# Final read and write of a fused two-block transformer kernel: residual tiles read without the last looped expert block, whose rows become a ninth tile

## What is computed

```python
x = x + gate_f * hierarchical_moe(h, ...)     # x before this: x3, [1024, 1024]
return rms_norm_2(x, final_g)

def hierarchical_moe(h, ...):                 # 2 of 32 experts for each token
    ...
    def run_block(args):                      # 128 slots of one expert
        tok, e = args
        xb = hf[jnp.minimum(tok, n_tok - 1)]
        return (jax.nn.silu(xb @ w_gate[e]) * (xb @ w_up[e])) @ w_down[e]
    out = lax.map(run_block, ...) * slot_gate
    return jnp.zeros((n_tok, dm)).at[slot_tok].add(out, mode='drop')
```

## Time and profile before

| what | us |
|---|---|
| median of 3 runs | 2104.06 (2104.06 to 2104.1) |
| the profiled execution | 2103.95 |
| its span | 2102.3 |
| TensorE busy | 2024.2 (96%) |
| VectorE busy | 1704.6 (81%) |
| ScalarE busy | 1232.5 (59%) |
| GpSimd busy | 445.4 (21%) |
| TensorE ends its last matmul | 2088.3 |

### The profile page before, as it was taken

How to read it: one execution, slowest core, us unless ns; L and a number is a source line. 1 busy time by engine, 2 the same in 40 slices (tenths; PEclk the granted TensorE clock), 3 DMA queues, 4 the chain that set the end, 5 groups by cost and what they waited for, 6 DMA issues and landing times.

```text
span 2102.3 us, 31575 instructions
## 1 busy us (share of the span) xinstructions
PE 2024.2 (96%) x9692; PEld 1673.5 (80%) x9692; DVE 1704.6 (81%) x1922; ACT 1232.5 (59%) x1438; POOL 445.4 (21%) x368
## 2 busy tenths in 40 slices
PE   5999999969999999999999999999999999999997
PEld 4888887858888888888788787888888888887874
DVE  6676756588999999999856455668999999999995
ACT  5311103226888888888644532224888888888874
POOL 2000001101000000100010353111444444444433
PEclk9999999969999999999999999999999999999999
DMA  9476754259999999999722112356999999999997
GB/s 353 142 235 227 253 196 161 110 210 337 390 392 401 392 398 392 400 390 383 280 66 60 32 41 102 119 191 227 386 384 379 375 382 374 363 381 364 380 350 274
DMA packets 201416, 592.52 MB, mean 282 GB/s; under 512 B 23936, under 2 KB 61076, under 8 KB 201341
## 3 DMA queue, kind: packets, MB, share of 16 engines
q1 hardware_dynamic: 177632, 527.50, 66.1%
q0 software_dynamic: 22640, 61.32, 10.1%
q10 hardware_dynamic: 1068, 2.73, 0.4%
HBM read 560.57 MB, written 50.91 MB: 291 GB/s over the span
## 4 chain that ended last, share of the span: by engine, by line
PE 77%; DMA 11%; DVE 8%; ACT 2%; issue 2%; POOL 0%; DVEq 0%; POOLq 0%; SPq 0%; ACTq 0%
PE ps L2467 23%; PE ps L2470 22%; PE ps L2468 22%; DMA ring<-in_w_expert_up 8%; DVE mL L2309 2%; PE ps L2812 1%; DMA ring<-in_ada_w 1%; PE ps L2981 1%; DMA ring<-in_w_expert_down 1%; ACT mH L1440 1%; PE ps L2588 1%; PE ps L2687 1%; DVE mL L2393 1%; PE ps L2676 1%; PE ps L2636 1%
## 5 line engine op out<-in xcount | busy, mean ns | idle before, releaser
L2309 DVE TENSOR_TENSOR mL<-ring,mH 128x1024 fp32r<-128x1024 f32 x384 | 480.8, 1292 | 21.8 <-ACT mH L1440 20.3
L1856 DVE TENSOR_TENSOR mL<-ring,mH 128x1024 fp32r<-128x1024 f32 x384 | 456.5, 1221 | 19.1 <-ACT mH L1231 5.2
L1231 ACT ACTIVATE mH<-ring 128x1024 fp32r<-128x1024 f32 x384 | 401.8, 1060 | 98.1 <-PE ps L2470 87.0
L1440 ACT ACTIVATE mH<-ring 128x1024 fp32r<-128x1024 f32 x384 | 396.4, 1056 | 70.0 <-PE ps L2470 24.3
L2467 PE MATMUL ps<-mH,xsH 128*128 128x512 f32 x1072 | 433.7, 405 | 2.9 <-DVE mL L2309 1.4
L2468 PE MATMUL ps<-mL,xsH 128*128 128x512 f32 x1072 | 418.0, 390 | 0.0
L2470 PE MATMUL ps<-mH,xsL 128*128 128x512 f32 x1072 | 376.8, 391 | 0.0
L2470 PEld LDWEIGHTS ps<-mH,xsL 128*128 128x128 f32 x1072 | 201.2, 188 | 45.0
L2467 PEld LDWEIGHTS ps<-mH,xsH 128*128 128x128 f32 x1072 | 201.7, 188 | 41.6 <-DVE mL L2309 1.6
L2468 PEld LDWEIGHTS ps<-mL,xsH 128*128 128x128 f32 x1072 | 202.0, 188 | 37.3
L948 POOL TENSOR_TENSOR xz<-xz,gate_ffn_row 128x340 f32<-128x340 f32 (+1 forms) x93 | 160.4, 1729 | 242.6 <-DVE mL L2309 216.7
(11 more groups left out here) (487 smaller groups left out, 3151.6 us busy)
## 6 DMA issues: line engine op xcount, KB each, us to landing
ring<-in_w_expert_gate SPq DMA_DIRECT2D x140, 512.0 KB, 12.2
ring<-in_w_expert_up SPq DMA_DIRECT2D x140, 512.0 KB, 12.2
ring<-in_w_expert_down SPq DMA_DIRECT2D x140, 512.0 KB, 12.9
ring<-in_moe_w_gate SPq DMA_DIRECT2D x128, 512.0 KB, 6.6
ring<-in_moe_w_up SPq DMA_DIRECT2D x128, 512.0 KB, 6.5
ring<-in_moe_w_down SPq DMA_DIRECT2D x128, 512.0 KB, 7.8
ring<-in_ada_w SPq DMA_DIRECT2D x96, 512.0 KB, 7.1
ring<-in_sc_w_in SPq DMA_DIRECT2D x24, 512.0 KB, 9.0
```

The source lines that it names most:

```text
L1231: act.activation(mH[:, wset, :], ring[:, slot, :], ACT.Copy).then_inc(S["m1_hi"], 1)
L1440: act.activation(mH[:, wset, :], ring[:, slot, :], ACT.Copy).then_inc(S["m2_hi"], 1)
L1856: dve.tensor_tensor(mL[:, wset, :], ring[:, slot, :], mH[:, wset, :].bitcast(F32), ALU.subtract).then_inc(S["m1_lo"], 1)
L2309: dve.tensor_tensor(mL[:, wset, :], ring[:, slot, :], mH[:, wset, :].bitcast(F32), ALU.subtract).then_inc(S["m2_lo"], 1)
```

## The change

- SyncE waits for the scatter before the last looped block's (`OUT1` without the 16) instead of its own, and reads the eight tiles without those rows.
- GpSimd gathers the last looped block's rows of x3 into `more_rows` (the buffer `gated`), VectorE adds the block's weighted result: the ninth tile. It is squared, its root made, and it is finished in place.
- The scatter into x3 stays, for tokens that are in the rest block too, and waits until all reads have landed (`x_in[t]` at 48).
- `patch(more_rows, tok_out[1])` and then `patch(ys[0], last_tok)` write over rows of `out`, one after the other.
- Finished tiles go to `xz[0]`, `acc`, `ring[0..3]`, `xz[0]`, `acc`, so that `ring[4..11]` keep the rest block's weights; tile 2 waits for the gate product, tiles 6 and 7 for the landing of writes 0 and 1.
- VectorE's `last_hidden` halves move behind tiles 4 and 6, `last_sum` behind all nine finishes; on ScalarE the Silu comes after square 3 and the copies of the hidden halves after square 7.
- The drain of the first looped block goes; one stands before the first gathers, one at the start of step 31.

```diff
-    out_rows = [ring[:, t, :] for t in range(NT)]
+    out_rows = [xz[:, 0, :], acc[:]] + [ring[:, u, :] for u in range(4)] + [xz[:, 0, :], acc[:]]
+    more_rows = gated
...
-        sp.wait_ge(m2_out[1], 16 * blocks + OUT1 + 16)
+        sp.wait_ge(m2_out[1], 16 * blocks + OUT1)
...
+        pool.drain()
         for e in range(2):
             tokens_known(0, e)
             gather2(0, e)
 
         def m2_step(q, r):
             s = 2 * q + r
+            if static(q) and s == E2 - 1:
+                pool.drain()
...
-            if static(b) and b == 0:
-                pool.drain()
             rows_back(b)
...
+        pool.wait_ge(m2_out[1], 16 * blocks + OUT1)
+        settle(pool)
+        pool.indirect_dma_start(out=more_rows, out_offset=None, in_=x3_dram,
+                                in_offset=bass.IndirectOffsetOnAxis(ap=tok_out[1][:, 0:1], axis=0),
+                                bounds_check=T - 1, oob_is_err=False).then_inc(xs_in[1], 16)
...
+        for t in range(NT - 1):
+            root(t)
         pool.wait_ge(S["ov_y"], blocks + 1 + past["ov_y"])
         settle(pool)
-        pool.wait_ge(m2_out[1], 16 * blocks + OUT1)
-        settle(pool)
+        for t in range(NT):
+            pool.wait_ge(x_in[t], 48)
         scatter_rows(ys[1], tok_out[1]).then_inc(m2_out[1], 16)
+        for t in (NT - 1, NT):
+            root(t)
         pool.wait_ge(m2_out[1], 16 * blocks + OUT1 + 16)
         settle(pool)
         pool.indirect_dma_start(out=ys[1], out_offset=None, in_=x3_dram,
...
+        pool.wait_ge(S["final_done"], NT + 1)
         for t in range(NT):
-            pool.wait_ge(S["var_final"], t + 1 + past["var_final"])
-            pool.tensor_tensor(stat[:, 10, t:t + 1], stat[:, 9, t:t + 1], neghalf[:, 0:1], ALU.pow).then_inc(S["rstd_final"], 1)
+            pool.wait_ge(x_in[t], 64)
+        patch(more_rows, tok_out[1])
         pool.wait_ge(S["close_dve"], 5)
         pool.tensor_tensor(stat[:, 11, 3:4], stat[:, 11, 2:3], neghalf[:, 0:1], ALU.pow).then_inc(S["last_root"], 1)
         pool.wait_ge(S["close_dve"], 6)
-        for t in range(NT):
-            pool.wait_ge(x_in[t], 64)
...
+        pool.wait_ge(S["last_out"], 16)
+        patch(ys[0], last_tok)
...
+            if t == 3:
+                act.wait_ge(S["close_mm"], 1)
+                act.activation(sg[:, 0:512], ps[:, 0, :], ACT.Silu).then_inc(S["close_act"], 1)
+        transposed(0)
+        act.wait_ge(S["ov_y"], blocks + 2 + past["ov_y"])
+        act.activation(squared[3], more_rows, ACT.Square, accum_out=stat[:, 11, 4:5]).then_inc(S["sq_final"], 1)
+        transposed(1)
...
         gated_rows(blocks, ys[1])
+        dve.wait_ge(xs_in[1], 16 * (E2 // 2 + 1) + XS_PAST)
+        dve.wait_ge(S["ov_y"], blocks + 1 + past["ov_y"])
+        dve.tensor_tensor(more_rows, more_rows, ys[1], ALU.add).then_inc(S["ov_y"], 1)
...
-        last_hidden(0)
         variance(0)
-        for t in range(6):
+        for t in range(NT):
             variance(t + 1)
             finish(t)
-            if t == 0:
-                last_hidden(1)
+            if t in (4, 6):
+                last_hidden((t - 4) // 2)
+        finish(NT)
         dve.wait_ge(m2_out[0], OUT0)
-        dve.wait_ge(xs_in[1], 16 * (E2 // 2 + 1) + XS_PAST)
+        dve.wait_ge(xs_in[1], 16 * (E2 // 2 + 2) + XS_PAST)
         last_sum(0)
         last_sum(1)
-        variance(7)
-        finish(6)
         dve.wait_ge(S["close_act"], 7)
         step(dve.tensor_tensor(stat[:, 11, 2:3], stat[:, 11, 0:1], stat[:, 11, 1:2], ALU.add))
...
-        finish(7)
```

More of the change, by code:

```diff
@@ L294, in build @@
         [("m1_hT_lo", 2 * E1), ("m2_hT_lo", E2), ("ov_l", 2 * NOVF)],
-        [("m2_y", E2 - 1), ("ov_y", NOVF)],
+        [("m2_y", E2 - 1), ("ov_y", NOVF + 1)],
         [("gate_in", 1), ("gate_rows", 2), ("gate_m", 1), ("neg_ready", 1), ("gcol_ready", 3)],
@@ L712, in _ @@
             sp.wait_ge(x_in[t], 64)
-        sp.wait_ge(S["last_out"], 16)
+        sp.wait_ge(S["last_out"], 32)
     @block.gpsimd
@@ L1041, in _, with patch @@
                                 bounds_check=T - 1, oob_is_err=False).then_inc(xs_in[1], 16)
+        def patch(src, row):
+            pool.indirect_dma_start(out=out, in_=src, in_offset=None,
+                                    out_offset=bass.IndirectOffsetOnAxis(ap=row[:, 0:1], axis=0),
+                                    bounds_check=T - 1, oob_is_err=False).then_inc(S["last_out"], 16)
+        pool.wait_ge(S["final_done"], NT + 1)
         for t in range(NT):
-            pool.wait_ge(S["var_final"], t + 1 + past["var_final"])
-            pool.tensor_tensor(stat[:, 10, t:t + 1], stat[:, 9, t:t + 1], neghalf[:, 0:1], ALU.pow).then_inc(S["rstd_final"], 1)
+            pool.wait_ge(x_in[t], 64)
+        patch(more_rows, tok_out[1])
         pool.wait_ge(S["close_dve"], 5)
@@ L1048, in _ @@
         pool.wait_ge(S["close_dve"], 6)
-        for t in range(NT):
-            pool.wait_ge(x_in[t], 64)
-        pool.indirect_dma_start(out=out, in_=ys[0], in_offset=None,
-                                out_offset=bass.IndirectOffsetOnAxis(ap=last_tok[:, 0:1], axis=0),
-                                bounds_check=T - 1, oob_is_err=False).then_inc(S["last_out"], 16)
+        pool.wait_ge(S["last_out"], 16)
+        patch(ys[0], last_tok)
     @block.scalar
@@ L2412, in _ @@
         gated_rows(blocks, ys[1])
+        dve.wait_ge(xs_in[1], 16 * (E2 // 2 + 1) + XS_PAST)
+        dve.wait_ge(S["ov_y"], blocks + 1 + past["ov_y"])
+        dve.tensor_tensor(more_rows, more_rows, ys[1], ALU.add).then_inc(S["ov_y"], 1)
         def variance(t):
             dve.wait_ge(S["sq_final"], t + 1 + past["sq_final"])
-            dve.tensor_scalar(stat[:, 9, t:t + 1], stat[:, 8, t:t + 1], 1.0 / D, EPS, ALU.mult,
-                              ALU.add).then_inc(S["var_final"], 1)
+            src, dst = (stat[:, 8, t:t + 1], stat[:, 9, t:t + 1]) if t < NT else (stat[:, 11, 4:5], stat[:, 11, 5:6])
+            dve.tensor_scalar(dst, src, 1.0 / D, EPS, ALU.mult, ALU.add).then_inc(S["var_final"], 1)
         def finish(t):
             dve.wait_ge(S["rstd_final"], t + 1 + past["rstd_final"])
-            dve.scalar_tensor_tensor(out=out_rows[t], in0=x_rows[t], scalar=stat[:, 10, t:t + 1], in1=final_row[:],
+            if t == 2:
+                dve.wait_ge(S["close_mm"], 1)
+            if t in (6, 7):
+                dve.wait_ge(x_in[t - 6], 64)
+            src, dst, root = ((x_rows[t], out_rows[t], stat[:, 10, t:t + 1]) if t < NT
+                              else (more_rows, more_rows, stat[:, 11, 6:7]))
+            dve.scalar_tensor_tensor(out=dst, in0=src, scalar=root, in1=final_row[:],
                                      op0=ALU.mult, op1=ALU.mult).then_inc(S["final_done"], 1)
```

14 lines of the change are left out of this document (7 added, 7 removed).

## The result

| kernel | median us | ratio to the kernel before (95%) |
|---|---|---|
| before | 2104.19 (21 runs) | |
| changed | 2107.68 (21 runs) | 1.0015 (1.0009 to 1.0021) |
| changed, second comparison (before there: 2104.15) | 2105.73 (11 runs) | 1.0006 (0.9997 to 1.0015) |
| changed, third comparison (before there: 2104.25) | 2107.15 (11 runs) | 1.0014 (1.0005 to 1.0023) |

The changed kernel is slower by 0.15%, 3.5 us between the medians; 2107.8 was predicted. That is within the 0.2% called "no change", and the interval reaches just over that bound. The two repeats put the difference at 1.6 and 2.9 us.

The account below looks back on a forecast made before the run. The tail was taken as a DMA stream of some 22 us, starting 7.1 us late. Gather there at 2096.3 plus 9.85 gave a span of 2106.15, plus 1.65 the time 2107.8 us; range 2102.5 to 2112.5.

Parts of the forecast that it names:

- The early reads: SyncE's eight reads of x3 start at 2067.4 instead of 2074.5, 7.1 us earlier; gain on this side 6.4 us.
- I move the landings by as much: Landings of the eight reads: 7.1 us earlier like their issue, the first at 2070.8, the last at 2081.3.
- The scatter: GpSimd's scatter into x3: starts at 2085.0 behind the root of tile 6, takes 8.0 us, lands at 2093.0.
- The gather: Rest block's gather from x3: starts at 2093.9 behind the scatter, takes 2.4 us, there at 2096.3.
- Rival C: Scatter and rest block's gather run as in idle queues, 4.8 + 2.4 us: time 2104.6 us; chance 0.18.
- B: Scatter and rest block's gather both at the loaded price, 10.2 + 7.2 us: 2115 us, slower for certain; chance 0.15.
- The tail behind the halves: From the first weighted half through last finish and patch to the end of the span: 9.85 us.
- The second patch: One more GpSimd write behind all tiles: 0.9 us of start and 2.4 us of landing, 3.3 us.
- TensorE's close: TensorE's transposes wait until 2082.3, its end moves from 2088.3 to about 2091.4, before 2096.3: 0.
- The rival with all of this work at half clock: TensorE's work from 2082.3 takes 18.8 us instead of 9.4: time 2111.2 us; part of B, chance 0.15 together.
- The drains: GpSimd loses a drain in the first looped block, gain 0, and gets two elsewhere: 0, at most 0.5 us.
- Rival E: The drain before step 31 outlasts its idle stretch, shifts gather and blocks 2 to 3 us: 2110 us; chance 0.05.

Follow-up runs that it names:

- Experiment 3: The changed kernel with the rest block's hidden halves multiplied behind tiles 2 and 4 instead of 4 and 6: 2106.8 us, ratio 1.0010.
- experiment 2: The changed kernel without the scatter of the last looped block, the rest block's gather ahead of all roots: 2102.48 us, ratio 0.9994.
- experiment 10: The kernel before with only the drains moved as in the change, run twice: 2102.02 us (0.9991) and 2102.70 us (0.9994).
- experiment 9: The changed kernel with the one drain back in the first looped block, as before the change: 2108.13 us, ratio 1.0014.

## Why the prediction was right, and where it was off

**The early reads: right in kind, too large.** The first read landed just before the first square, 41.9 and 42.3 us behind W1; predicted was 2070.8, which is 40.6. Of the gain of 7.1 us 5.3 to 5.7 were there (47.67 to 42.33 and 41.93). The step that failed is "I move the landings by as much": the landing time of 3.4 us came from a queue that had run empty, and now it is 7.8, or 4.7 where the reads are issued as late as the forecast has them, because SyncE's queue still holds the rest block's weights. The last read had landed when its square started, 51.2 and 52.0 behind W1, where the forecast had it land at 51.1: of a first read that is 1.7 and 1.3 us late, a last one that is 0.2 and 0.9 late is left, as the reads follow each other faster than before. The last tile of the output has landed 63.1 and 63.9 us behind W1, against 61.8 in the forecast, and is not last either way.

**The scatter: right.** Forecast: behind the root of tile 6, at 54.8 behind W1, landing in 8.0. Measured: 53.8 and 53.3, landing in 8.1 and 8.7; the start was early by 1.0 and 1.5, 0.4 of it since from the root's end to the scatter it took 0.6 us and not 1.0, the rest since the root itself ended earlier. It is loaded by the writes, as said: 5.2 us without them. The Trainium skill, "DMA: Bandwidth & Descriptors", section "Queues, rings and completion order", has each DMA engine take turns between queues a packet at a time. These runs fit that, though the turns themselves are not seen in them: what runs beside it, not its own bytes, makes 5.2 into 8.1, and the same load, put beside the gather, makes 3.0 into 5.2.

**The gather: right, small miss.** 3.0 us instead of 2.4. The first weighted half was forecast at 66.06 and started at 65.92 and 66.10. Rival C, which has both at the idle price, falls by the 8.1; of B the first half, both at the loaded price, falls by the 3.0.

**The tail behind the halves: right.** 9.94 and 9.90 us against 9.85.

**The second patch: right.** Forecast on the path only as the last write, which replaces the one of before; it is. The first patch is hidden in the gap of GpSimd.

**TensorE's close: the event right, the end right.** The forecast had it end at 61.2 behind W1 and "0" for the path; it ended at 63.8 and 62.6, part of it at half clock, and still 2.1 and 3.5 us ahead of the halves. Its wait for the first hidden half, forecast at 2.8 us, is 5.73 in the second comparison's profile, where TensorE was done with the loop earlier, and 2.60 in the third's; the clock fell to 0.50 behind both. Experiment 3 shows that it isn't the bound, experiment 2 that it is the next one, by 4.1 us. The rival with all of this work at half clock has a sum that doesn't add up: 2082.3 + 18.8 is 2101.1, not 2099.7, which would make it 2112.6 us.

**The drains: wrong.** They were put at "gain 0", since the scatter that the old one held back "has until the second block's weighting at 2051 to land". It hadn't: VectorE's row of that weighting, before the change, carries a wait for this very scatter:

```profile
2051.37 1.28 DVE L2379 SCALAR_TENSOR_TENSOR xz<-ps,slot_w,gate_ffn_row 128x1024 f32<-128x1024 f32 x1 [0.44 <-DMA x_dram<-xz,tok_out]
```

In the profile of before this wait is short, 0.44 us, only because a stretch at half clock had delayed the weighting by 2.7 us (21.13 behind W1, against 18.43); in a profile without this (changed, old drain) it is 3.37 us, and the clock is at half about 10 us later, in 2060 to 2064. Moved drains are worth 1.2 to 1.6 us in the kernel before and 1.7 to 1.9 in the changed one, in profiles; the medians say 1.6 to 2.4 us, at the edge of their intervals. The prediction gives as a sign of being wrong that anything before 2060 has moved by over 1 us. It has: the first looped pass's scatter starts 9.1 us behind W1 in both profiles of the changed kernel, against 12.3, and the second weighting 18.4 (second comparison) against 21.1. Rival E, that the new drain delays the looped blocks by 2 to 3 us, falls: the drain before step 31 ends at 2006.2 in the second comparison's profile (its row is in the last section), and GpSimd goes on with

```profile
2006.39 5.18 POOL L949 TENSOR_TENSOR xz<-xz,gate_ffn_row 128x344 f32<-128x344 f32 x3 [10.15 <-DVE mL L2331]
```

0.2 us behind the drain's end, though the bracket names VectorE. That is 11.9 us behind the start of its scatter against 11.1 before, 0.8 us later, and the gather of the first pass is issued 2.7 us ahead of W1 in both kernels (2027.53 and 2026.74).

**Was the total right by luck?** The price of the tail was not, the whole in part. With the drains in the same places everything else costs 4.0, 3.7 and 4.5 us between the medians (experiment 10), where 3.85 was forecast. The drains, put at 0, give back 1.6 to 2.4, so that the whole is 3.5, 1.6 and 2.9 us above before, where the forecast had 3.7 (2107.8 less 2104.06); that the first comparison came out right next to it is in part chance. Within the tail, too, errors make up for each other: the third comparison's profile has W3 at 37.13, as the forecast assumed (37.11), and ends at 76.00 against 75.91, with a first square 1.4 us late, a scatter 1.5 us early, and a landing and a gather 0.7 and 0.6 us too long. In the second comparison's profile W3 comes 2.6 us earlier and the end all the same. With the old drain the changed kernel's profile ends 5.7 us behind before (77.72 against 72.06), outside the bound for "no change", and its median lies 4.0 us above before, just inside.

**What stays open.** Whether TensorE's clock falls in the first looped pass is not settled by the length of its wait for the gather at 2037: with moved drains it fell in three of eleven profiles, at waits of 1.61, 1.67 and 1.71 us, and didn't at 1.65 and 1.66. That the half clock in 2060 to 2064 of experiment 9 comes of VectorE's wait is argued from the order of events, in one profile. Why the time up to W1 varies by 5 us is open. That the moved drains make the kernel before faster rests on two comparisons, whose intervals reach 1.0000 and 1.0003. What the forecast's early reads would bring without the weights in the queue was not tried.

## What to carry over

Moving a read ahead of the work that its data lacks only pays if what has to come later (here scatter, gather, patch) doesn't end up behind everything that the read has set going: ask first what is last once the work is rearranged, and price it at the load that it will meet there, 8 us and not 5. A read that is issued early, on a queue still busy with earlier transfers, lands behind them: here 2.7 us of earlier issue gave nothing. And a wait of 0.44 us in a profile can be a wait of 3.4 us that something else happens to cover: before writing "gain 0" behind a held instruction, read who waits for it in the very row.

## What was not expected of the hardware

A drain on GpSimd took long in all three places where it stood: 13.9 us in the first looped pass of before, and in the changed kernel (DRAIN on GpSimd's queue, ns and start us):

```profile
L993 POOLq DRAIN  x1: 8381/8381/8381, 1421.3 to 1421.3; - x1
...
L1001 POOLq DRAIN  x1: 11932/11932/11932, 1994.3 to 1994.3; - x1
```

At 1421.3 GpSimd has already waited for its last DMA and has eight small operations under way or left, the last of which ends at 1422.4; the drain takes 8.4 us. What it waits for there is not shown; a DMA that GpSimd issued it is not.

The end of the changed kernel hardly depends on when TensorE was done with the loop: W3 at 34.47 or 37.13, the end at 75.86 or 76.00. With the old drain, and W3 at 40.33, it is at 77.72.
